# A two-layer mixture-of-experts block: the second layer's expert loop written out in small pieces, and the modulation jobs set in other places

## What is computed

```python
def first_block(x, c, ctx, ...):                 # x 512 x 1024 tokens, ctx 256 x 1024
    for l in range(2):
        mod  = silu(c)     @ w_ada[l] + b_ada[l]      # 6 groups of 1024: shift, scale, gate, twice
        modc = silu(c_ctx) @ w_ada[l] + b_ada[l]
        h = modulate(rmsnorm(x, g_mix[l]), sh1, sc1)
        x = x + gt1 * latent_mixer(h @ w_in[l], ...)  # attention, windowed attention, conv, gates
        h2 = modulate(rmsnorm(x, g_ffn[l]), sh2, sc2)
        x = x + gt2 * expert_choice_ffn(h2, w_router[l], w_e_gate[l], w_e_up[l], w_e_down[l])
        if l == 0:
            ...                                       # the same for ctx

def expert_choice_ffn(h, w_router, w_g, w_u, w_d):    # 16 experts, each takes its 2n/16 best tokens
    aff = softmax(h @ w_router)
    gate, idx = top_k(aff over tokens, cap)           # cap 64 for x, 32 for ctx
    xs = h[idx]
    y = (silu(xs @ w_g) * (xs @ w_u)) @ w_d           # each 1024 x 1024 per expert
    return zeros.at[idx].add(y * gate)
# then second_block: one more attention layer on x
```

## Time and profile before

| what | us |
|---|---|
| median of 3 runs (3381.45 to 3385.0) | 3384.51 |
| the profiled execution, its own time | 3384.78 |
| its span, first to last instruction | 3382.8 |
| PE busy | 3170.2 |
| DVE busy | 1081.0 |
| ACT busy | 641.1 |
| transfers, mean over the span | 163 GB/s |

### The profile page before, as it was taken

How to read it: one execution, slowest core, us unless ns; L and a number is a source line. 1 busy time by engine, 2 the same in 40 slices (tenths; PEclk the granted TensorE clock), 3 DMA queues, 4 the chain that set the end, 5 groups by cost and what they waited for, 6 DMA issues and landing times. The chain is left out here.

```text
span 3382.8 us, 35291 instructions
## 1 busy us (share of the span) xinstructions
PE 3170.2 (94%) x13725; PEld 1554.2 (46%) x13725; DVE 1081.0 (32%) x1554; ACT 641.1 (19%) x1120; POOL 16.7 (0%) x35
## 2 busy tenths in 40 slices
PE   7999999999887999999989999999789889889998
PEld 4665555555543333333334655444334334244544
DVE  5754545455532011111127553011300010017441
ACT  3145520000011111111121452000111001021151
POOL 1000000000000000000000000000000000000000
PEclk9999999999998999999999999999899999999999
DMA  7020023343414878787860201222188989962200
GB/s 228 1 75 26 2 93 115 128 155 116 158 57 162 306 280 306 283 303 283 306 160 0 75 20 38 75 75 93 50 324 342 410 348 363 394 213 70 67 1 26
DMA packets 299287, 551.80 MB, mean 163 GB/s; under 512 B 62744, under 2 KB 137768, under 8 KB 299016
## 3 DMA queue, kind: packets, MB, share of 16 engines
q1 hardware_dynamic: 297232, 546.53, 45.4%
q0 software_dynamic: 1600, 3.20, 0.3%
q10 hardware_dynamic: 312, 0.05, 0.0%
HBM read 547.63 MB, written 2.10 MB: 163 GB/s over the span
## 5 line engine op out<-in xcount | busy, mean ns | idle before, releaser
L772 PE MATMUL ps<-hT,ring 128*128 128x512 f32 (+1 forms) x2128 | 797.0, 532 | 17.6 <-ACT hT L1331 16.6
L772 PEld LDWEIGHTS ps<-hT,ring 128*128 128x128 f32 x2128 | 405.2, 191 | 394.6 <-issue 369.3
L1085 PE MATMUL ps<-ring,hT 128*64 128x512 f32 x1536 | 358.2, 602 | 64.2 <-DMA ring<-in_w_e_up 35.2
L1064 PE MATMUL ps<-ring,hT 128*64 128x512 f32 x1536 | 350.8, 598 | 1.5 <-ACT hT L1331 1.5
L1085 PEld LDWEIGHTS ps<-ring,hT 128*64 128x64 f32 x1536 | 100.3, 137 | 312.0 <-issue 161.0
L2005 DVE SCALAR_TENSOR_TENSOR xT<-ps,mod,xT 128x512 f32<-128x512 f32 x96 | 63.5, 662 | 498.7 <-PE ps L1171 281.1
L1064 PEld LDWEIGHTS ps<-ring,hT 128*64 128x64 f32 x1536 | 101.8, 136 | 235.6 <-issue 235.1
L772 PE MATMUL ps<-obuf,ring 128*128 128x512 f32 (+1 forms) x512 | 198.4, 540 | 0.9 <-issue 0.9
L788 PE MATMUL ps<-hT,ring 128*128 128x512 f32 (+1 forms) x448 | 191.4, 555 | 0.3 <-DVEq L1316 0.2
L1070 PE MATMUL ps<-ring,hT 128*32 128x512 f32 x1536 | 184.7, 598 | 0.0
L1663 DVE SCALAR_TENSOR_TENSOR vbuf<-ring,silc,vbuf 128x1024 f32<-128x1024 f32 x140 | 179.9, 1285 | 6.1
(11 more groups left out here) (240 smaller groups left out, 2635.9 us busy)
## 6 DMA issues: line engine op xcount, KB each, us to landing
ring<-in_w_e_gate SPq DMA_DIRECT2D x128, 512.0 KB, 6.9
ring<-in_w_e_up SPq DMA_DIRECT2D x128, 512.0 KB, 7.0
ring<-in_w_e_down SPq DMA_DIRECT2D x128, 512.0 KB, 7.1
ring<-in_w_e_gate SPq DMA_DIRECT2D x64, 1024.0 KB, 10.6
ring<-in_w_e_up SPq DMA_DIRECT2D x64, 1024.0 KB, 10.7
ring<-in_w_e_down SPq DMA_DIRECT2D x64, 1024.0 KB, 10.7
ring<-in_w_in SPq DMA_DIRECT2D x49, 1024.0 KB, 5.5
ring<-in_w_ada SPq DMA_DIRECT2D x48, 1024.0 KB, 6.5
```

Source lines behind the costliest of these rows:

```text
L772: mm = pe.matmul(ps[:, b + a:b + e], lhs[:, k, :], rhs[:, k, a:e], start=k == 0, stop=k == nk - 1)
L1064: mm = pe.matmul(ps[e * CX:(e + 1) * CX, b + pair * 512:b + (pair + 1) * 512], lhs[:, k, s0:s0 + CX], expert_dst(0, slot, e)[:, k % 2, :], ...
L1085: mm = pe.matmul(ps[e * CX:(e + 1) * CX, b + h * 512:b + (h + 1) * 512], lhs[:, k, s0:s0 + CX], expert_dst(1, slot, 0)[:, e, h * 512:(h + ...
```

## The change

For layer 1 the loop is gone: all four rounds are written out. One list, `PAIR_STEPS`, sets PE's order. The `out` of round i - 1 is cut into 8 pieces that stand before chunks 2, 4, ... 16 of round i, `gt` into two before chunks 18 and 19, the gather of round i + 1 into 8 before chunks 20 to 38, and `ht` stand before chunks 28 and 37. The pieces use two PSUM banks in turn (`SIDE_BANK`), the chunks' products and `ht` the other six (`pair_bank`). The gathered tokens have two buffers (`xs_pair`). Every chunk has its own semaphore step. The last round has no gather, and its `out` follows its last chunk. Layer 0's experts keep their loop (`experts_first`), and the router's part is a function of its own, unchanged.

In layer 0's dense stretch modulation jobs follow only jobs that are not `rb`, `rr` or `lg`: 40 `acc` are spread evenly over the first 56 of those 60, `rsum` stands two such jobs behind its group's last `acc`, `adag` three. `macc` has two sets of buffers, the second in `kbuf` and `prob`.

```diff
-        macc = vbuf[:, 0:2 * D].rearrange("p (w f) -> p w f", w=2)
+        macc = [[vbuf[:, 0:D], vbuf[:, D:2 * D]],
+                [kbuf[:, 0:D], pr[:].rearrange("p k t -> p (k t)")[:, 0:D]]]
...
+        xs_pair = [hT[:, n * 2 * KD * P:(n + 1) * 2 * KD * P].rearrange("p (k s) -> p k s", k=KD) for n in range(2)]
...
-            for group in [(m, g) for m in range(DEPTH) for g in range(6) if (m, g) >= (0, 2)]:
-                todo += [("acc",) + group + (q,) for q in range(4)] + [("rsum",) + group, ("adag",) + group]
-            order = []
+            todo = [("acc",) + group + (q,) for group in groups for q in range(4)]
+            count, passed, share = len(todo), 0, sum(1 for j in jobs if j[0] not in SHORT) - 4
+            order, due = [], []
             for j in jobs:
                 order.append(j)
-                if todo:
-                    order.append(todo.pop(0))
+                if j[0] in SHORT:
+                    continue
+                passed += 1
+                while due and due[0][0] <= passed:
+                    order.append(due.pop(0)[1])
+                while todo and (count - len(todo)) * share < passed * count:
+                    k = todo.pop(0)
+                    order.append(k)
+                    if k[3] == 3:
+                        due += [(passed + 2, ("rsum",) + k[1:3]), (passed + 3, ("adag",) + k[1:3])]
...
+            at = {}
+            if i > 0:
+                for d in range(KD):
+                    at.setdefault(2 * d + 2, []).append(("out", i - 1, d))
+            at[18], at[19] = [("gt", i, 0)], [("gt", i, 1)]
+            if i + 1 < ROUNDS:
+                for d, r in enumerate((20, 22, 24, 26, 28, 30, 34, 38)):
+                    at.setdefault(r, []).append(("in", i + 1, d))
+            at.setdefault(28, []).append(("ht", i, 0))
+            at.setdefault(37, []).append(("ht", i, 1))
...
+                    at = PIECES.index(p)
+                    b = SIDE_BANK[at % 2]
+                    if at >= 2:
+                        need(evacuated(PIECES[at - 2]), PIECES[at - 2])
+                    if kind == "in":
+                        need(pair_slots, i)
...
+                    elif kind == "gt":
+                        need(pair_weighted, i)
...
+                    else:
+                        need(pair_out, (i, 1))
+                        need(pair_gates, ("gt", i, 1))
...
+                    mm.then_inc(pair_used.sem, 1)
+                    chunk_end[n] = (pair_used.sem, pair_used.at[step[1:]])
...
-                if q == 0 and (l, g) > (0, 2):
-                    V.read(("rsum",) + ((l, g - 1) if g else (l - 1, 5)))
+                n = ADA_GROUPS.index((l, g))
+                if q == 0 and n >= 2:
+                    V.read(("rsum",) + ADA_GROUPS[n - 2])
...
+                for i in range(ROUNDS):                      # DVE, layer 1
+                    if i + 1 < ROUNDS:
+                        V.need(piece_full, ("in", i, KD - 1))
+                        selected(i + 1, selx, None, pair_slots)
+                    outs = list(range(KD)) if i > 0 else []
+                    for d in outs[0:3]:
+                        added(i - 1, d)
+                    hidden(i, 0, "eg")
+                    for d in outs[3:7]:
+                        added(i - 1, d)
+                    hidden(i, 0, "eu")
+                    for d in outs[7:]:
+                        added(i - 1, d)
+                    if i + 1 < ROUNDS:
+                        V.need(piece_full, ("gt", i, 1))
+                        selected(i + 1, gselx, selx, pair_weighted)
+                    hidden(i, 1, "eg")
+                    hidden(i, 1, "eu")
```

More of the change, by code:

```diff
@@ new lines, in program @@
+        SIDE_BANK = [3072, 3584]
+        WEIGHT_ORDER = [("eg", 0), ("eu", 0), ("eg", 1), ("eu", 1), ("ed", 0), ("ed", 1)]
+        PAIR_STEPS = []
+        PAIR_STEPS += [("piece", ("in", 0, d)) for d in range(KD)]
+        for i in range(ROUNDS):
+            pieces_at = side_pieces(i)
+            for r in range(len(WEIGHT_ORDER) * KD):
+                PAIR_STEPS += [("piece", p) for p in pieces_at.get(r, [])]
+                PAIR_STEPS.append(("chunk", i) + WEIGHT_ORDER[r // KD] + (r % KD,))
@@ new lines, in program @@
+        PAIR_STEPS += [("piece", ("out", ROUNDS - 1, d)) for d in range(KD)]
+        PIECES = [s[1] for s in PAIR_STEPS if s[0] == "piece" and s[1][0] != "ht"]
+        pair_used = event("pair_chunk_used", [s[1:] for s in PAIR_STEPS if s[0] == "chunk"])
+        piece_full = event("piece_full", PIECES)
+        pair_turned = event("pair_hidden_turned", [s[1] for s in PAIR_STEPS if s[0] == "piece" and s[1][0] == "ht"])
+        pair_copied = event("pair_hidden_copied", [("ht", i, p) for i in range(ROUNDS) for p in range(2)])
@@ L1585, in experts @@
-                if l == 0:
-                    A.n += ROUNDS
+                    copied.then_inc(act_step, 1)
+                    act.wait_ge(act_step, i + (A.n + 1))
+                    release(("gt", 0))
+                    sigmoid(0)
+                    b = read(("gt", 1))
+                    sc.copy(gTc, ps[:, b:b + NC]).then_inc(gT_ready, 1)
+                    act.wait_ge(gT_ready, i + 1)
+                    release(("gt", 1))
+                    sigmoid(1)
+                    turned(0)
```

493 lines of the change are left out of this document (281 added, 212 removed).

## The result

The changed kernel takes 3318.97 us, median of 4 runs (3318.61 to 3320.36); the kernel before, run beside it, 3383.66. The ratio is 0.9814, 95% interval 0.9802 to 0.9827. Forecast were 3321, and 3311 to 3337 as the range: faster, by 64.7 us where 63.7 were worked out. The profiled execution of after has a span of 3318.6 us.

A forecast was written before the change was run, and what follows sets the result against it. Layer 1's experts were taken as bound by interrupted weight transfers, the end of layer 0's dense stretch by PE. Gains of 40.6 + 1.8 + 3.4 + 17.9 = 63.7 us from 3384.51 gave 3321 us, range 3311 to 3337.

The forecast's parts named there:

- Rounds written out, 40.6: Layer 1's experts: unbroken transfers cut first chunk to last chunk's end from 525.9 to 481.3 us plus 4 for fetches.
- The lag stays near 3 us: Layer 1's rounds: PE, with pieces between chunks, stays about 3 us behind the weight transfers, so these go on.
- PE may lag a landing by 8.1 us: Layer 1's six weight slots: PE may be 8.1 us late before transfers pause, 15.3 - 5.45 - 1.74.
- Rival E: SP still sees slots in twos: start loses 1.7 us, allowed lag 6.4; inside the forecast, no chance of its own.
- Fetches, 4 us: Layer 1's written-out rounds: about 12 instruction fetches delay chunks by 4 us, between 1.5 once and 18 in all.
- Rival A: Written-out rounds: all instruction fetches hit one DMA engine, costing 18 us instead of 4; 3335 us, chance 0.12.
- Rival C: Layer 1's stream holds only 371 GB/s, not 2.55 us a chunk; rounds gain nothing; 3361 us, chance 0.04.
- Start, 1.8: Start of layer 1's experts: earlier gather, `gt` off the way and a shorter last ACT copy save 1.8 us.
- End, 3.4: End of layer 1's experts: no fifth-round gather, a smaller last add, less a 1.2 us `ye` wait: 3.4 us saved.
- Modulation, 17.9: Layer 0's dense stretch: new job places remove 12.56 us of waits before `rsum` and slow running behind: 17.9 us saved.
- the 0.7 to come back: Layer 0's dense stretch: first `wout` waits for DVE to add in the last `branch`, giving back 0.7 us.
- Rival D: Slower than before: unhidden waits at pieces stop PE before most chunks and its clock falls; 3445 us at 0.75, chance 0.03.

The follow-up runs named there:

- half of the weights: The changed kernel, loading only the first expert's half (0.5 MB of 1 MB) of each of layer 1's expert chunks, all PE instructions kept: 3277.52 us.
- the run of the experts alone: Layer 1's experts written out as in the change, modulation jobs in old places with one pair of accumulators as in the kernel before: 3334.66 us, ratio 0.9857.

## Why the prediction was right, point by point

- **Rounds written out, 40.6: measured 40.4.** Chunk 191 was to land at 12.7 + 183 x 2.55 = 479.4, with 4 us for fetches 483.4. It starts at 2927.18 - 2443.59 = 483.6. The working behind that sum was less exact than the sum. The step is 2.555 and not 2.55, which is 0.9 over 183 chunks; the rest, 3.3, is lateness: 1.1 more by the end of the first round (the second round starts 98.25 us behind chunk 10 where 38 steps are 97.1), 0.3 in the second, 1.5 in the third (124.12 against 48 x 2.555 = 122.6), 0.2 in the last. That the sum comes out within 0.2 us is luck in part, as the bullet on fetches shows.
- **"The lag stays near 3 us": wrong.** Two chunks and an `out` piece cost 5.50 us and not 5.20; two chunks and a gather piece 5.51. The piece was sized by a row in which 32 matmuls stand in a row (rows 2), where a change of shape costs nothing; the run with pieces in twos puts the change at 0.36 us. A round of PE's work is 119.0 us (half of the weights) and not 114.3. The lag reaches 7.0 us in after.
- **"PE may lag a landing by 8.1 us": somewhat too much.** The block of `out` pieces shows 7.5 absorbed, and with pieces in twos the stream pauses at 7.3. The term too small is "issued 2.9 + 2.55 us before it lands": in a full stream chunk 84 of after, issued 6.4 us before its landing, is in time, and with pieces in twos it would have had to land 6.0 us behind its issue and was 0.7 late. With 6.4 for 5.45 the same sum gives 7.2. Both errors lean the same way: a margin of 5 us was forecast, and next to nothing is left. Rival E was judged harmless with "the lag allowed shrinks to 6.4, still over 3"; with 7.0 of lag it costs 3.9 us of the stage, of which 2.3 show in the time. It stayed inside the forecast because a ring that overflows loses about the excess and no more, once a round.
- **Fetches, 4 us: right in kind, too large in size, and made good by another error.** By the landings fetches of PE cost 2.3 us in after. The rest of the 4.2 us over 481.3 is the step, 2.559 and not 2.55 (1.7 us), and 0.2 at the start: a guess too large and a step too short cancel. The losses do not come every 40 us: four of 15 fetches cost 0.1 to 1.1 us and eleven nothing, so neither "1.5 once" nor "1.5 each" is what happens. The 1.5 us of the third round fall while PE is late, but not at its greatest lag: the slots had been free for long.
- **Rival A: its mechanism exists, but not for PE's blocks.** GpSimd's blocks of 8 KB cost 0.48 us each on balance and add up over a full stream. Had PE's done so, 15 of them would have cost 7 us or, by their size, twice that. The chance of 0.12 was not too high.
- **Rival C: refuted.** 409 GB/s (406 in the last round) and share 1.03 hold over 480 us. By the Trainium skill (DMA: Bandwidth & Descriptors, Where 436 GB/s comes from) a core reads about 358 GB/s from HBM; the trace contradicts that as a limit here.
- **Start, 1.8: measured 1.4.** The terms as given add up to 2.45 and not to 1.8 (1.2 + 0.97 + 0.58 - 0.3), so the forecast is nearer than its working. The gather starts 1.2 earlier as forecast, and the way from its end to the first chunk is 0.9 shorter. What was put at nothing is the gather itself: it takes 16.22 us and not 15.56, at a granted clock of 0.86 and not 0.89. SP's first issue went from 3.91 to 1.98 us as worked out (2.17), which is part of the rounds.
- **End, 3.4: measured 2.9** (the terms gave 3.3; 20.15 from rows 3 to the norm's first matmul at 3010.69, against 17.24). The wait for the `ye` copy was forecast at 1.2 and is 1.20.
- **Modulation, 17.9: measured 18.2.** The two waits are gone and the clock is 1.00 behind them. Of the 0.7 to come back, 0.93 stand before the first `wout` (at 882.30). The runs show the cause: the second buffer alone gives nothing, the places do. What the slow running behind a wait costs is not fixed: 1.85 and 1.41 us were added up for the two `wout`, and with the same waits the run of the experts alone has 11.26 and 11.41 us, 0.7 and 0.8 over 10.59.
- **Rival D**, slower: no wait of PE over 0.75 us is left in the stage, and the clock is 1.00 throughout. Nothing of it appeared, even with the `out` pieces in a block.
- **Stages not touched** gave 1.4 us more, which no term held: the stretch between the dense stage and layer 1's experts became shorter. One piece is seen: the second pair of pieces in the gather of layer 0's experts took 1.06 us and 2.57 us in before and takes 0.67 and 1.89 in after, with a granted clock of 0.70 there in before and 0.98 in after. Differences of the clock in places that no edit touches made up to 5.8 us between other runs (behind the last chunk: 389.5 us in after, 383.7 with the old places and both pairs of accumulators), so 1.4 is nothing that a forecast could hold, and a time within 2 us of the forecast is in part luck.

## What to carry to other kernels

When transfers are the bound, work out how late the computing engine may be before a transfer must wait for a slot, and place everything else in pieces so small that the lateness stays below it; then the pieces are free, and a block of them costs about what lies above, once per block (13.2 us of lag, 7.5 absorbed, 5.7 lost). Leave a margin: at a lag of 7.0 us 0.3 us at most were lost, at 7.3 already 0.7 to 1.1. Size a piece where it will stand, between matmuls of another shape, and not in a row of its like; and keep small jobs that wait for another engine behind jobs of PE that last longer than that engine's last step, which took both waits away, where an additional buffer alone took away none.

## What the runs showed of the hardware

- A full stream of 1 MB chunks holds 2.555 us a chunk, 409 GB/s (406 in the last round), for 480 us, while PE is busy 89 to 98% of the time (108.25 of 122.17, 120.15 of 122.94).
- Code fetched by GpSimd is not free beside such a stream: 0.48 us on balance for each block of 8 KB, 0.5 to 0.7 where one is seen alone, though most of its packets take 0.31 to 0.32 us and 34 blocks are 0.28 MB, 0.7 us of the stream. PE's blocks of 16 KB, whose packets take 1.03 to 1.16 us, cost 0.15 us each on the mean of 15, but unevenly: 0.11, 0.38, 0.86 and 1.08, and the others nothing.
- Going from a chunk's matmuls (128*64 in the rows) to a piece's (128*128) and back costs 0.36 us a time, semaphores included, seen as 5.50 against 5.32 us for the same instructions.
- Waits of 0.6 us before every chunk leave PE's granted clock at 1.00; a single one of 7.05 us brings 0.80 over 25 us in before and again in the run with the old places and both pairs of accumulators, and 0.86 in the run of the experts alone.
- The granted clock of one and the same stretch differs between runs: 0.66 in after and 1.00 in the run of the experts alone, over 20 us of the second block that no edit touches. From the end of the last chunk to the end of the span the two take 389.5 us and 385.3.
